# One stream of attention groups in the first block, with the index key's tile projected first

## What is computed

```
h = rms(x) * ln1 * (1 + sc1) + sh1
p = h @ w_in             # columns: qa ka va qi ki wi qb kb vb qc kc vc, heads of 64
qa, ka = rope(rms(qa)), rope(rms(ka));   qc, kc = rope(rms(qc)), rope(rms(kc))
qi, ki = rope(qi), rope(ki)
oa = dsa(qa, ka, va, qi, ki, wi)         # 4 heads: scores of 4 index heads pick the 128 keys per query
ob = stick_breaking(qb, kb, vb)          # 4 heads: weights from cumulated log sigmoids over all earlier keys
oc = swa_sinks(qc, kc, vc, sinks)        # 8 heads: window of 128 keys, with a sink
x = x + g1 * (rms(concat(oa, ob, oc)) * g_out) @ w_o
x = x + g2 * swiglu(rms(x) * ln2 * (1 + sc2) + sh2)
```

```
score = sum_h wi[h] * relu(qi[h] . ki);  sel = top_k(score over keys <= query, 128)
o = softmax(qa . ka[sel] / 8) @ va[sel]
```

## Time and profile before

| | us |
|---|---|
| median of three runs (lowest, highest) | 3133.84 (3128.38, 3138.25) |
| the profiled execution | 3130.37 |
| its span | 3128.6 |
| PE busy in the span | 2908.3 (93%) |
| DVE busy | 1787.2 (57%) |
| ACT busy | 756.2 (24%) |
| POOL busy | 931.1 (30%) |

### The profile page before, as it was taken

One profiled execution on the slowest core, in us unless ns is written; L12 is line 12 of the kernel. 1 busy time (PEld: TensorE's weight loads), 2 busy tenths in 40 slices (PEclk: granted clock), 3 DMA queues, 4 the chain that ended last, 5 costly groups with the idle time before them and its releaser, 6 DMA issues.

```text
span 3128.6 us, 33693 instructions
## 1 busy us (share of the span) xinstructions
PE 2908.3 (93%) x12126; PEld 2133.1 (68%) x12126; DVE 1787.2 (57%) x3803; ACT 756.2 (24%) x1781; POOL 931.1 (30%) x794
## 2 busy tenths in 40 slices
PE   8888999999997899999989988999999998899997
PEld 4354688888544578888854456888884454688886
DVE  2673469388367447938854545877824634551433
ACT  2354310000235431000022353201112335320111
POOL 0301224443330124444412202344440400344442
PEclk9989999999998799999989988999999998899998
DMA  6115034244221013434421101254421210122221
GB/s 256 64 61 215 28 138 166 101 148 170 91 80 61 1 55 121 175 108 156 154 76 56 61 27 68 108 183 186 156 100 57 59 50 23 40 94 96 81 81 54
DMA packets 45412, 313.28 MB, mean 100 GB/s; under 512 B 5424, under 2 KB 5552, under 8 KB 31040
## 3 DMA queue, kind: packets, MB, share of 16 engines
q1 hardware_dynamic: 42912, 306.88, 27.0%
q10 hardware_dynamic: 2304, 4.20, 0.6%
q0 software_dynamic: 32, 0.07, 0.0%
HBM read 298.53 MB, written 2.10 MB: 96 GB/s over the span
## 4 chain that ended last, share of the span: by engine, by line
PE 70%; DVE 18%; ACT 6%; issue 3%; DMA 1%; POOL 1%; DVEq 0%; SPq 0%; ACTq 0%; POOLq 0%
PE bank L1114 39%; PE bank L1094 9%; PE bank L1440 7%; PE bank L1168 3%; DVE nw L2067 3%; PE bank L1264 2%; DVE sel L2304 2%; DVE m L2303 1%; PE bank L1307 1%; DVE SPT L2368 1%; ACT SPT L1756 1%; PE bank L1294 1%; PE bank L1229 1%; PE bank L1567 1%; DMA sel<-in_mod_pieces 1%
## 5 line engine op out<-in xcount | busy, mean ns | idle before, releaser
L1000 POOL TENSOR_TENSOR SPT<-ring 128x512 f32<-128x512 f32 (+2 forms) x140 | 175.2, 1252 | 956.3 <-DMA ring<-in_slabs 493.0
L1114 PE MATMUL bank<-U,ring 128*128 128x256 f32 x1728 | 412.2, 384 | 10.8 <-DVE U L2101 10.5
L1114 PEld LDWEIGHTS bank<-U,ring 128*128 128x128 f32 x1728 | 332.8, 193 | 58.4 <-DVE U L2101 12.5
L2067 DVE SCALAR_TENSOR_TENSOR nw<-sel,c,nw 128x256 f32<-128x256 f32 x504 | 321.7, 638 | 31.2 <-DMA sel<-in_mod_pieces 13.5
L1114 PE MATMUL bank<-U,SPT 128*128 128x256 f32 x1296 | 312.5, 381 | 3.0 <-POOL SPT L1005 3.0
L1114 PEld LDWEIGHTS bank<-U,SPT 128*128 128x128 f32 x1296 | 247.4, 191 | 37.7 <-POOL SPT L1005 4.4
L1114 PE MATMUL bank<-hT,SPT 128*128 128x256 f32 x1088 | 257.1, 379 | 0.0
L1440 PE MATMUL bank<-hT,ring 128*128 128x512 f32 x544 | 249.7, 607 | 7.1 <-ACT hT L1873 7.1
L2127 DVE TENSOR_TENSOR rb<-bank,nw 128x256 f32<-128x256 f32 x108 | 45.5, 422 | 355.9 <-PE bank L1114 259.1
L1114 PE MATMUL bank<-hT,ring 128*128 128x256 f32 x1088 | 246.1, 379 | 0.0
L1114 PEld LDWEIGHTS bank<-hT,ring 128*128 128x128 f32 x1088 | 207.0, 190 | 28.0 <-DMA ring<-in_slabs 0.3
(11 more groups left out here) (344 smaller groups left out, 4501.9 us busy)
## 6 DMA issues: line engine op xcount, KB each, us to landing
ring<-in_slabs SPq DMA_DIRECT2D x86, 2048.0 KB, 8.0
sel<-in_mod_pieces SPq DMA_DIRECT2D x144, 512.0 KB, 4.5
ring<-in_slabs SPq DMA_DIRECT2D x8, 1536.0 KB, 7.0
ring<-in_slabs SPq DMA_DIRECT2D x8, 1280.0 KB, 8.3
tab<-U SPq DMA_DIRECT2D x40, 128.0 KB, 2.0
U<-in_slabs SPq DMA_DIRECT2D x2, 2048.0 KB, 22.5
tmp<-nw ACTq DMA_DIRECT2D x16, 256.0 KB, 2.9
ring<-in_slabs SPq DMA_DIRECT2D x2, 1808.0 KB, 11.7
```

Source lines behind the costliest of these rows:

```text
L1000: pool.tensor_tensor(e1, a21, a22, ALU.add).then_inc(*pool_order.up())
L1114: mm = pe.matmul(into[j][:, c:c + HALF], lhs[:, k, :], rhs[:, k, :], start=(begin and k == 0), stop=(end and k == kp - 1))
L2067: ins = dve.scalar_tensor_tensor(a, w[:, k, :], c[:, j:j + 1], a, ALU.mult, ALU.add)
```

## The change

Tile 2 (the index key, with its norm) is projected first, and stick-breaking's first query and key tiles (6, 8) before the selected heads' (4, 5). V blocks are projected in the order 1, 2, 3, 0, each beside the index scores of the query block that needs its wi, with three top-k rounds after each. Then a single `woven` merges ten dense tiles, all fourteen groups, the remaining rounds, stick-breaking, the modulation slabs and the first half of the output projection. The waits follow: index scores wait for the rotation of the last index tile, a DVE index sum waits for its own V block alone, the copy of the shared key is issued behind the `tab` copy of tile 0, and slabs are released by the tiles that are now last in them. The host packs weight columns by `TILES1`. Cut to its core:

```diff
-TILES1 = (0, 1, 2, 10, 12, 13, 14, 15, 4, 5, 6, 7, 8, 9)
+TILES1 = (2, 0, 1, 10, 12, 13, 14, 15, 6, 8, 4, 5, 7, 9)
+V_ORDER = (1, 2, 3, 0)
-TURNED_BEHIND = {("v", 0): ROPED[:2], ("kq", 0): ROPED[2:3], ("qa", 0): ROPED[3:6], ("qb", 0): ROPED[6:]}
+TURNED_BEHIND = {("v", 0): ROPED[:3], ("kq", 0): ROPED[3:4], ("qa", 0): ROPED[4:7], ("qb", 0): ROPED[7:]}
@@ order1
-        sums = [("pss", TILES1[m - 1])] if 0 <= m - 1 < NT1 and TILES1[m - 1] in NORMED else []
+        sums = [("pss", TILES1[m - 1])] if 0 <= m - 1 < NT1 and TILES1[m - 1] in NORMED and m != 4 else []
-    for m in range(6):
-        if (l, m) == (0, 2):
+    for m in range(4):
+        if (l, m) == (0, 1):
             o.append(("tables",))
         o += [st for part in tile(m) for st in part]
-        if m == 3:
-            o += [("rope", KI)] + [("projv", i) for i in range(QT)]
-        if m >= 3:
-            o += [("idx", m - 2, hp) for hp in range(2)]
-        if m >= 4:
-            o += [st for chunk_ in rounds[:8] for st in chunk_]
-            rounds = rounds[8:]
+        if m == 2:
+            o += [("projv", V_ORDER[0])]
+    o += [("rope", TILES1[2])]
+    for i in range(1, QT):
+        o += [("idx", i, hp) for hp in range(2)] + [("projv", V_ORDER[i])]
+        o += [st for chunk_ in rounds[3 * i - 3:3 * i] for st in chunk_]
+        if i == 1:
+            o += [("pss", KC)]
+    rounds = rounds[9:] + [[("seldone", i)] for i in range(1, QT)]
     dense = []
-    for m in range(6, NT1 + 2):
+    for m in range(4, NT1 + 2):
         dense += tile(m)
-    o += woven((-0.03, 0.92, dense), (0.37, 1.01, group_slots(range(NC1))),
-               (0, 1.15, rounds + [[("seldone", i)] for i in range(1, QT)]))
...
-    o += woven((0, 0.96, stick_slots()), (0.08, 0.95, group_slots(range(NC1, len(GROUPS1)))),
-               (0, 0.55, mods), (0.55 if l == 0 else 0.1, 1, [[("wo", 0, n)] for n in range(KT)]))
+    o += woven((-0.01, 0.6, dense), (0.22, 0.95, group_slots(range(len(GROUPS1)))), (0, 0.22, rounds[:18]),
+               (0.22, 0.5, rounds[18:]), (0.42, 0.94, stick_slots()), (0.57, 0.79, mods),
+               (0.78 if l == 0 else 0.68, 1.02, [[("wo", 0, n)] for n in range(KT)]))
@@ SP
-                        if k in (roped_at[KI], roped_at[KC] + 1):
+                        if k in (roped_at[KI] + 1, roped_at[KC] + 1):
@@ PE
-                        pe.wait_ge(*s1["rope"].after(l, roped_at[KI] + 1))
+                        pe.wait_ge(*s1["rope"].after(l, roped_at[QI + 1] + 1))
@@ DVE
-                        if i == 1 and hp == 0:
-                            for j in range(QT):
-                                dve.wait_ge(*bk1.taken(l, ("projv", j)))
+                        if hp == 0:
+                            dve.wait_ge(*bk1.taken(l, ("projv", i)))
```

More of the change, by code:

```diff
@@ L400 @@
           + [("wo", s) for s in range(2)] + ffn_slabs(1))
-LAST1 = {("qi", 0): ("proj", 10), ("v", 0): ("projv", 3), ("kq", 0): ("proj", 15), ("qa", 0): ("proj", 7),
+LAST1 = {("qi", 0): ("proj", 10), ("v", 0): ("projv", V_ORDER[-1]), ("kq", 0): ("proj", TILES1[7]), ("qa", 0): ("proj", TILES1[11]),
          ("qb", 0): ("proj", 9)}
@@ L950, in _ @@
                             sp.dma_start(tab[e:P:2, k % 2, :], PT[1 - e:P:2, t, :]).then_inc(halves_turned[k % 2], 16)
-                        if k in (roped_at[KI], roped_at[KC] + 1):
-                            t = SHARED[k != roped_at[KI]]
+                        if k in (roped_at[KI] + 1, roped_at[KC] + 1):
+                            t = SHARED[k != roped_at[KI] + 1]
                             sp.wait_ge(*s1["rope"].after(l, roped_at[t] + 1))
@@ L1261, in _ @@
                         for k in (2 * part, 2 * part + 1):
-                            if n == 0:
+                            if n == TILES1[0]:
                                 pe.wait_ge(*s1["h"].after(l, k + 1))
@@ L1313, in _ @@
                         pe.wait_ge(*s1["ba"].after(l, h + 1))
-                        pe.wait_ge(*bk1.taken(l, ("projv", QT - 1)))
+                        pe.wait_ge(*bk1.taken(l, ("projv", V_ORDER[-1])))
                         for j in range(QT):
@@ L2712, in slab, with tile_columns @@
         w = inputs["w_in"][l]
-        if kind == "qi":
-            return tiled(heads(np.concatenate([w[:, 384:704], w[:, 256:320], w[:, 1988:2116]], axis=1)))
+        def tile_columns(n):
+            at = {0: 384, 1: 512, 2: 640, 4: 0, 5: 128, 6: 708, 7: 836, 8: 964, 9: 1092, 10: 1988,
+                  12: 1476, 13: 1604, 14: 1732, 15: 1860}[n]
+            if n == KI:
+                return heads(np.concatenate([w[:, at:at + HD], w[:, 256:320]], axis=1))
+            return heads(w[:, at:at + P]) if n in ROPED else w[:, at:at + P]
+        if kind in ("qi", "kq", "qa", "qb"):
+            return tiled(np.concatenate([tile_columns(n) for n in TILES1 if SLAB_OF_TILE[n][0] == kind], axis=1))
         if kind == "v":
             return cols("w_in", (320, 384), (704, 708), (1220, 1476), (2116, 2244))
-        if kind == "kq":
-            return tiled(heads(w[:, 1476:1988]))
-        if kind == "qa":
-            return tiled(np.concatenate([heads(w[:, 0:256]), w[:, 708:964]], axis=1))
-        if kind == "qb":
-            return cols("w_in", (964, 1220))
         if kind == "wo":
```

## The result

The changed kernel takes 3174.91 us (median of 4 runs, 3169.62 to 3182.14) against 3132.15 (4 runs, 3128.38 to 3138.25): ratio 1.0135 [1.0111, 1.0158], 43 us slower where 32 faster was forecast. The profiled execution took 3182.14 us with a span of 3180.4, 51.8 over that of before; it is the slowest of its four, 7 us above their median, so some 9 of the 51.8 us belong to the two executions and not to the kernels.

A forecast was written before the change was run, and what follows sets the result against it. TensorE, busy 93% of the span, was taken as the bound, with its idle time and slow clock winnable. Gains of 15 and 17 us in layers 0 and 1 took 3130.4 to 3098.4; plus 3.4, forecast 3102, range 3072 to 3136.

The forecast's parts named there:

- The two signs of being wrong: VectorE's last round later than 215, or TensorE's waits behind the last dense tile over 20 us a layer.
- The signs of being right: Among others, layer 0's stretch: 25 to 32 us idle, clock 0.95 or more; last round at 190 to 205.
- Step 1, the opening: Start of each layer: index key first, V projections singly; VectorE's index sums start at 77.0, 18 us earlier.
- Step 2, VectorE's middle: Index sums to last round: long mask wait cut up, about 16 us idle and 5 of clock kept per layer.
- the queue of 104 + 15.6 us: VectorE's work and norm waits from 77 to the last round, put at 197 in place of 236.
- The rule cited in the prediction: VectorE and GpSimd share SBUF interfaces and contend; more meetings in norms add about 2 us a layer.
- The clock term: Slow-clock loss kept: 5 us in each middle, 5 and 10 in the late parts, 4 at layer 0's start.
- Step 3, cover in the late part: Dense tiles cover stick-breaking's start; idle and clock kept are 11 + 5 us in layer 0, 14 + 10 in layer 1.
- The slower one: Norms at tiles 15, 4, 5: VectorE stalls on ScalarE's order, products held by the bank; 3156, chance 0.15.
- The saving is given back later: Late part: TensorE waits at stick-breaking's end as before, only early clock won; about 3128, no change, chance 0.13.

The follow-up runs named there:

- e4: Changed kernel with the groups started later (0.27 in place of 0.22): 3164.9 us, ratio 1.0100 to the kernel before.
- e5b: Changed kernel with layer 0's modulation slabs spread over 0.58 to 0.88 and its output projection from 0.86: 3181.8 us, ratio 1.0151 to the kernel before.
- e2: Opening of the kernel before, with the changed kernel's single stream and order of tiles: 3177.6 us, ratio 1.0148 to the kernel before.
- e3: Changed kernel with stick-breaking started later (0.6 to 0.96 in place of 0.42 to 0.94): 3152.2 us, ratio 1.0058 to the kernel before.
- e11: Kernel before with the new opening and the changed kernel's order of tiles, keeping two streams: 3147.3 us, ratio 1.0048 to the kernel before.
- e12: Changed kernel with stick-breaking from 0.6 and the groups from 0.27, sums in their old bank: 3168.6 us, ratio 1.0114 to the kernel before.
- e14: Changed kernel with stick-breaking from 0.6 and tiles 4 and 5 ahead of 6 and 8 again: 3155.0 us, ratio 1.0070 to the kernel before.
- e15: New opening, two streams, last dense tile moved to the second, slabs at 0.2 to 0.75, output projection from 0.7: 3145.5 us, ratio 1.0039 to the kernel before.
- e6b: Changed kernel with sums of squares in the small transposed outputs' bank: 3165.1 us, ratio 1.0102 to the kernel before.
- e13: e11 with sums of squares in the small transposed outputs' bank: 3134.9 us, ratio 1.0011 to the kernel before.

## Why the prediction was wrong

**The sum, term by term.** TensorE's idle time was to fall from 37 to 28 us in layer 0 (16 + 11 + 1) and from 37 to 30 in layer 1; it rose to 46 in both. The clock was to cost 14 us in layer 0 (4 + 5 + 5) and 20 in layer 1. By 0.13 of 310.7 us busy and 0.12 of 282.2 it cost an estimated 40 and 34 (before, 20 and 30). Two steps made this, VectorE's middle and the cover in the late part. The two signs of being wrong did not catch it: the last round at 212.6 stayed under 215, and 18.5 and 17.1 us of idle time behind the last dense tile under 20. The signs of being right did: idle time 46 in place of 25 to 32, clock 0.87 in place of 0.95.

**Step 1, the opening, was right.** DVE starts at 75.70 (forecast 77.0), the key is in time, and by itself the opening wins: 8 us over both layers.

**Step 2, VectorE's middle, failed twice.** First a wait was missing from it. I let TensorE wait for masks alone. But local group 0 needs the rotated tile 13, and I brought the groups forward in the list without asking when VectorE gives that rotation. TensorE reached group 0 at 129.8 and VectorE, with rounds ahead of it, finished at 140.3: 10.7 us in each layer, as long as the wait removed. (In the kernel before, scores start 106 us behind the first tile; in the changed kernel 103. Bringing them forward won 3 us and held the dense tiles for 10.7.) e4, which starts the groups later, halves the wait to 5.7 and is 11 us faster over two layers. Second, the queue of 104 + 15.6 us was too short: last round at 212.6, not 197. Its busy part was right (102.3 us from 75.7 to 213.3); the waits were not. Between its first index sum and its last round, VectorE waits 15.4 us for roots, 4.9 for GpSimd in norms, 7.2 for ScalarE in a group's output, and 6.6 for rotations, copies and banks: 34 where I had 15.6. A further 0.4 us on each of 8 norm passes (1490 ns mean, 1096 before) comes from meeting GpSimd more often, as at 121.91, where it takes 1.73 beside GpSimd's pass. The rule cited in the prediction held, with 3 us.

**The clock term was mis-sized.** Up to the last round I took 9 us in layer 0 (4 + 5) and 10 in layer 1. From the first to the last dense tile the clock is 0.89 and 0.92, by busy time an estimated 20 and 14 us, where before it was 0.94 and 10 us a layer. A part of layer 0's 20 is this one execution. Behind the wait of 5.83 us, from 184.8 to 190.6, TensorE ran 21 us at 0.50, which cost some 10. The same steps in e5b, whose list is the same up to there, behind a wait of 4.89:

```profile
186.50:207.50 21.00, 20.02 (x82) 13.11 (x82) 13.29 (x36) 11.70 (x28) 2.63 (x2) 0.86 0.04 14
```

The changed kernel, e2, e3, e4, e5b, e11, e12, e14 and e15 have this wait in both layers, with 4.3 to 8.2 us. Behind sixteen of the eighteen the next 21 us are at 0.80 to 0.87, some 3 us lost; behind two, layer 0's here and in e2, at 0.50. A late wait of 5 us thus cost 8 as a rule, and 15 in this execution. For the late part I took 5 and 10 us; the same estimate gives 21 and 19, before 9 and 20. Layer 0's is again unsure: the clock behind its last dense tile is 0.83 here, 0.81 in e5b and 0.90 in e6b. The Trainium skill, TensorE: Matmul & The Clock Gate, A second HAM failure mode: psum-queue depth-cycling, says of a bf16 matmul kernel that pauses often between groups while it cycles through PSUM banks that its clock falls and rises again. The traces agree in that the clock was low behind every one of these waits; no run here shows what decides how long it stays low.

**Step 3, cover in the late part, failed as an argument.** I kept three quarters of 14 and 18 us of idle time because dense tiles would cover the start of stick-breaking. From the last dense tile on, TensorE idles 18.5 us in layer 0 and 17.1 in layer 1, before 20.4 and 20.5: the cover saved 2 to 3. Up to that tile it idles 28 us a layer, before 16. In layer 0 stick-breaking started 36 us earlier (159 behind the first tile, before 195), the last dense tile came 31 us later (213, before 182), and the stretch behind that tile was 144 in both, with 35 matmul records less and a clock of 0.83 in place of 0.93. In layer 1 the tile came 27 us later and the stretch behind it was 10 shorter. Of the 31 and 27 us I estimate 12 as idle time, 10 (in part that one execution) and 5 as clock, and the rest, some 10, as stick-breaking's own matmuls, which had only changed sides. So what was moved among the dense tiles held them up by more than it saved behind them. e3 shows the price: 24 us for stick-breaking's place alone. e3 and e14 are still 27 to 30 us behind the opening alone. That lies in the dense part: 189 to 194 us a layer in place of 173 to 175, with 22 to 26 us of idle time in place of 10 to 11. The waits for rotation 13 and for a root, 10.7 + 5.8 in e3 and 10.7 + 8.2 in e14, are 16 to 19 of it. No run takes these waits away and leaves the rest as it is, so that they are the whole cause is argued, not shown.

**The rivals.** The slower one, with 0.15, named ScalarE's order, the held bank and tiles 15, 4 and 5, and gave 3156. Its mechanism is there: TensorE waits for a root once a layer, not six times, and VectorE's waits between its first index sum and its last round are 34 us, near the 35 it named, 20 of them at norms. Taking TensorE's wait away gave 12 us in two streams (e11 to e13), and in the changed kernel 10, not clear of noise (e6b). It is not the main loss. "The saving is given back later" is true of the opening alone only in part: 8 us stay. The range ended at 3136, since I bounded the middle's idle time by norms and had no bound for a wait on rotations or for clock behind many small waits.

## What to carry over

Before a consumer is moved ahead in a list that all engines share, work out when its last operand is ready on the slowest engine's queue, as was done here for the index key and not for tile 13. Weaving latency chains among dense work is no gain by itself: each step that isn't ready holds the dense work as well, and the slow clock behind it adds to the price (mostly 3 us here behind a wait of 5, in two cases 10); two places that are each better alone can be worse together when they share banks. And before 15 us of clock in a profile are explained, profile the same kernel again.

## What was not expected of the hardware

- The same 253 matmuls took 44.9 us at a mean granted clock of 0.96 in two executions and 59.9 at 0.66 in a third, with 3.9 us idle in the faster ones and 2.0 in the slower.
- TensorE can be busy and stay at the 1.2 GHz level: 20.42 of 21 us at 0.50 in the changed kernel, in tile projections and value products behind a wait of 5.83 us. In e5b the same steps behind a wait of 4.89 ran at 0.86.
